# Input splits first, sums of squares last, at the start of a decoder-step kernel

## The reference

```
xn = rmsnorm(x, norm1_g)
z = einsum('btd,de->bte', xn, w_in)
rg_x, rg_y, q, k, v, g_lr, g_out, m_a, m_b = split(z)
```

## Time and profile before

| | |
|---|---|
| three runs, median | 1937.57 us |
| lowest and highest of them | 1936.34 and 1939.11 us |
| the profiled execution | 1936.35 us |
| its span in the profile | 1934.5 us |
| TensorE busy | 1901.1 us |
| VectorE, ScalarE, GpSimd busy | 925.8, 563.5, 41.7 us |

### The profile page before, as it was taken

The page is one execution under the profiler, slowest core; times in us unless marked ns, Lnnn a source line. Parts: engine busy times, 40 slices in busy tenths (PEclk is TensorE's granted clock), DMA queues, the critical chain, the costliest instruction groups (busy, mean ns, idle before and its releaser), DMA issues. The chain is left out here.

```text
span 1934.5 us, 28895 instructions
## 1 busy us (share of the span) xinstructions
PE 1901.1 (98%) x11890; PEld 1872.9 (97%) x11890; DVE 925.8 (48%) x1063; ACT 563.5 (29%) x627; POOL 41.7 (2%) x30
## 2 busy tenths in 40 slices
PE   7999999999999999999999999999999999999997
PEld 6999899999999999999999999999999999999997
DVE  5221277778854222332244455545453545454556
ACT  4010255665542111211132332222121212121215
POOL 2000000000000000000000000000000000000033
PEclk9999999999999999999999999999999999999998
DMA  5221123222211111311131111111111111111112
GB/s 195 88 91 44 44 68 135 99 81 97 93 66 43 44 54 43 132 44 43 50 136 44 56 45 46 53 45 44 45 44 46 53 45 44 44 44 55 44 52 88
DMA packets 48169, 127.13 MB, mean 66 GB/s; under 512 B 6952, under 2 KB 20008, under 8 KB 48080
## 3 DMA queue, kind: packets, MB, share of 16 engines
q1 hardware_dynamic: 27744, 88.39, 13.4%
q10 hardware_dynamic: 20352, 37.64, 5.5%
HBM read 108.14 MB, written 18.14 MB: 65 GB/s over the span
## 5 line engine op out<-in xcount | busy, mean ns | idle before, releaser
L414 PE MATMUL acc<-xn_hi,w_hi 128*128 128x346 f32 (+1 forms) x2520 | 551.6, 327 | 16.4 <-DVE xn_lo L1172 12.4
L414 PE MATMUL acc<-xn_lo,w_hi 128*128 128x346 f32 (+1 forms) x2520 | 540.2, 323 | 0.0
L414 PE MATMUL acc<-xn_hi,w_lo 128*128 128x346 f32 (+1 forms) x2520 | 538.9, 322 | 0.0
L414 PEld LDWEIGHTS acc<-xn_hi,w_hi 128*128 128x128 f32 x2520 | 425.8, 190 | 22.2 <-issue 13.3
L414 PEld LDWEIGHTS acc<-xn_lo,w_hi 128*128 128x128 f32 x2520 | 428.1, 189 | 0.0
L414 PEld LDWEIGHTS acc<-xn_hi,w_lo 128*128 128x128 f32 x2520 | 427.0, 189 | 0.0
L776 ACT ACTIVATE w_hi<-w_raw 128x1024 fp32r<-128x1024 f32 x147 | 154.3, 1050 | 468.5 <-PE acc L414 468.4
L1194 DVE TENSOR_TENSOR w_lo<-w_raw,w_hi 128x1024 fp32r<-128x1024 f32 x147 | 180.0, 1224 | 177.8 <-ACT w_hi L776 177.7
L1576 DVE TENSOR_TENSOR residual<-acc,residual 128x1032 f32<-128x1032 f32 x56 | 69.0, 1231 | 100.2 <-PE acc L414 100.2
L414 PE MATMUL acc<-act_hi,w_hi 128*128 128x344 f32 x504 | 108.2, 323 | 2.3 <-DVE residual L1576 2.3
L414 PE MATMUL acc<-act_hi,w_lo 128*128 128x344 f32 x504 | 107.6, 321 | 0.0
(11 more groups left out here) (218 smaller groups left out, 1990.6 us busy)
## 6 DMA issues: line engine op xcount, KB each, us to landing
w_raw<-in_w SPq DMA_DIRECT2D x153, 512.0 KB, 3.5
ha_scratch<-rg_gelu_ha ACTq DMA_DIRECT2D x8, 519.0 KB, 2.7
h<-ha_scratch ACTq DMA_DIRECT2D x8, 519.0 KB, 6.6
residual<-in_x ACTq DMA_DIRECT2D x8, 519.0 KB, 9.0
gla_qk_pair<-qk_scratch ACTq DMA_DIRECT2D x8, 512.0 KB, 4.5
smp_v_rows<-smp_v_scratch ACTq DMA_DIRECT2D x8, 512.0 KB, 5.7
out_gla_sample<-smp_state ACTq DMA_DIRECT2D x8, 512.0 KB, 3.2
smp_state<-in_gla_state ACTq DMA_DIRECT2D x7, 512.0 KB, 4.8
```

Of the source, the lines that this page charges most:

```text
L414: mm = nc.tensor.matmul(acc[g][:, n, 0:cw], w[s][:, t * P:(t + 1) * P], x[:, c0 + n * cw:c0 + (n + 1) * cw], start=a, stop=z)
```

## The change

Unit 0's transfer is cut in two, a head of two tiles (256 columns) with a semaphore of its own, and the rest, behind the parameters. Block 3 goes ahead of unit 1's weights. SyncE issues units 2 and 3 when units 0 and 1 are split, and only then the parameters and states. GpSimd's two splits are gone: ScalarE and VectorE split unit 1 behind block 2 and unit 2 in the middle of the squares. ScalarE does all eight high halves first, then squares into four buffers; VectorE does all eight low halves first, then the additions. After the fourth square ScalarE waits for unit 0, copies its 16 rows out of PSUM without the factor, which frees the bank, and splits unit 2's high half; VectorE multiplies the copy by the factor later, in place (`low_ready`). The sums over the partitions move back by one tile on TensorE. At the feed-forward's start, the residual's reload shares semaphores with the first load of the input.

The diff, without the declarations of semaphores:

```
@@ sync
-            sp.dma_start(raw[0], I["w"][0]).then_inc(w_loaded[0], 16)
+            sp.dma_start(raw[0][:, 0:HEAD], I["w"][0][:, 0:HEAD]).then_inc(head_loaded, 16)
             sp.dma_start(prm, I["params"]).then_inc(prm_loaded, 16)
+            sp.dma_start(raw[0][:, HEAD:], I["w"][0][:, HEAD:]).then_inc(w_loaded[0], 16)
             sp.dma_start(blk(X1, 1), I["x"][1]).then_inc(x_loaded[1], 16)
+            sp.dma_start(blk(X1, 3), I["x"][3]).then_inc(x_loaded[3], 16)
             sp.dma_start(raw[1], I["w"][1]).then_inc(w_loaded[1], 16)
-            for k in range(3, KB, 2):
+            for k in range(5, KB, 2):
                 sp.dma_start(blk(X1, k), I["x"][k]).then_inc(x_loaded[k], 16)
+            for s in range(2):
+                sp.wait_ge(w_split[s], 1)
+                sp.dma_start(raw[s], I["w"][2 + s]).then_inc(w_loaded[s], 16)
...
-            with sp.Fori(1, N_UNITS // 2) as i:
+            with sp.Fori(2, N_UNITS // 2) as i:
@@ gpsimd
-            split(0, 1)
-            split(1, 0)
@@ tensor
-                if k == 0:
+                if (g, k) == (0, 0):
+                    pe.wait_ge(head_split, 1)
+                elif (g, k) == (0, HEAD // P) or (g, k) == (1, 0):
                     pe.wait_ge(w_split[s], 1)
...
-                if (g, k) == (1, KB - 3):
+                if (g, k) == (1, KB - 2):
                     pe.wait_ge(sum1_done, KB)
                     norm_sum(xc, 0, sb6, sum1_mm)
                     norm_sum(xc, 1, sb7, sum1_mm)
-                if (g, k) == (1, KB - 2):
+                if (g, k) == (1, KB - 1):
                     pe.wait_ge(lnr1_done, 1)
                     norm_sum(xc, 2, sb6, sum1_mm)
...
-                pe.wait_ge(acc_free[0], 1)
+                pe.wait_ge(low_ready, 1)
                 zg_piece(0, NMETA, 0)
@@ scalar
-            act.wait_ge(w_loaded[0], 16)
-            nc.scalar.activation(whi[0], raw[0], ACT.Copy).then_inc(w_hi_done[0], 1)
+            act.wait_ge(head_loaded, 16)
+            nc.scalar.activation(whi[0][:, 0:HEAD], raw[0][:, 0:HEAD], ACT.Copy).then_inc(head_hi_done, 1)

             act.wait_ge(prm_loaded, 16)
             for k in range(KB):
                 act.wait_ge(x_loaded[k], 16)
                 nc.scalar.activation(blk(XH, k), blk(X1, k), ACT.Identity, scale=par("g1", k)).then_inc(xh1_done, 1)
-                if k >= 2:
-                    act.wait_ge(sum1_done, k - 1)
-                nc.scalar.activation((rt, it)[k % 2], blk(X1, k), ACT.Square).then_inc(sq1_done, 1)
+                if k == 0:
+                    act.wait_ge(w_loaded[0], 16)
+                    nc.scalar.activation(whi[0][:, HEAD:], raw[0][:, HEAD:], ACT.Copy).then_inc(w_hi_done[0], 1)
+                if k == 2:
+                    w_high(1)
+            for k in range(KB):
+                if k >= 4:
+                    act.wait_ge(sum1_done, k - 3)
+                nc.scalar.activation(sq1[k % 4], blk(X1, k), ACT.Square).then_inc(sq1_done, 1)
+                if k == 3:
+                    act.wait_ge(unit_done[0], 1)
+                    nc.scalar.activation(view3(glr[0:RANK]), acc[0][0:RANK, :, 0:NW], ACT.Copy).then_inc(acc_free[0], 1)
+                    w_high(2)
@@ vector
-            dve.wait_ge(w_hi_done[0], 1)
-            nc.vector.tensor_tensor(wlo[0], raw[0], whi[0].bitcast(F32), ALU.subtract).then_inc(w_split[0], 1)
+            dve.wait_ge(head_hi_done, 1)
+            nc.vector.tensor_tensor(wlo[0][:, 0:HEAD], raw[0][:, 0:HEAD], whi[0][:, 0:HEAD].bitcast(F32), ALU.subtract)\
+                .then_inc(head_split, 1)
...
             for k in range(KB):
                 dve.wait_ge(xh1_done, k + 1)
                 nc.vector.scalar_tensor_tensor(blk(XL, k), blk(X1, k), par("g1", k), blk(XH, k).bitcast(F32),
                                                ALU.mult, ALU.subtract).then_inc(xl1_done, 1)
+                if k == 0:
+                    dve.wait_ge(w_hi_done[0], 1)
+                    dve.wait_ge(head_split, 1)
+                    nc.vector.tensor_tensor(wlo[0][:, HEAD:], raw[0][:, HEAD:], whi[0][:, HEAD:].bitcast(F32), ALU.subtract)\
+                        .then_inc(w_split[0], 1)
+                if k == 2:
+                    w_low(1)
+            for k in range(KB):
                 dve.wait_ge(sq1_done, k + 1)
                 if k == 0:
-                    nc.vector.tensor_copy(xc, rt).then_inc(sum1_done, 1)
+                    nc.vector.tensor_copy(xc, sq1[0]).then_inc(sum1_done, 1)
                 else:
                     dve.wait_ge(sum1_done, k)
-                    nc.vector.tensor_tensor(xc, xc, (rt, it)[k % 2], ALU.add).then_inc(sum1_done, 1)
+                    nc.vector.tensor_tensor(xc, xc, sq1[k % 4], ALU.add).then_inc(sum1_done, 1)
+                if k == 3:
+                    w_low(2)
...
             dve.wait_ge(r1_done, 1)
-            evacuate(0, 0, 0, 0, glr[0:RANK, :], RANK)
+            dve.wait_ge(acc_free[0], 1)
+            nc.vector.tensor_tensor(glr[0:RANK, :], glr[0:RANK, :], rms[0:RANK, :], ALU.mult).then_inc(low_ready, 1)
```

More of the change, by code:

```diff
@@ L73 @@
 N_UNITS = U_FFN + UB + FB
+HEAD = 2 * P
 U_LAST = N_UNITS - GRP
@@ L200, in build @@
         sqsum = T[2]
+        sq1 = (rt, it, av, th)
         act_bytes = (2 * GRP * CB + 31) // 32 * 32
@@ L264, in build @@
         V3 = V.rearrange("p (k c) -> p k c", k=KB)
+        head_loaded, head_hi_done, head_split, low_ready = (
+            sem(n) for n in ("head_loaded", "head_hi_done", "head_split", "low_ready"))
         w_loaded, w_hi_done, w_split, unit_done = sems("w_loaded"), sems("w_hi_done"), sems("w_split"), sems("unit_done")
@@ L309, in build @@
         mgh_done, mgl_done = sem("mgh_done"), sem("mgl_done")
-        xr_loaded = sems("xr_loaded", KB)
         sq2_done, sum2_done, sum2_mm, lnr2_done, r2_done, xh2_done, xl2_done = (
@@ L774, in w_high @@
                 act.wait_ge(w_loaded[s], 16 * n + 16)
-                act.wait_ge(unit_done[s], n)
+                if u >= 2:
+                    act.wait_ge(unit_done[s], n)
                 nc.scalar.activation(whi[s], raw[s], ACT.Copy).then_inc(w_hi_done[s], 1)
@@ L1065, in _ @@
                     for m in range(KB):
-                        act.dma_start(blkl(X2, m), I["x"][m][:, late]).then_inc(xr_loaded[m], 16)
+                        act.dma_start(blkl(X2, m), I["x"][m][:, late]).then_inc(x_loaded[m], 16)
                 act.wait_ge(ma_done, KB if k == KB - 1 else k + 1)
@@ L1163, in plain, with w_low @@
                 dve.wait_ge(ones_done, 1)
-            dve.wait_ge(w_hi_done[0], 1)
-            nc.vector.tensor_tensor(wlo[0], raw[0], whi[0].bitcast(F32), ALU.subtract).then_inc(w_split[0], 1)
+            def w_low(u, per=0, i=0):
+                s, n = slot_of(u), nth(u, per, i)
+                dve.wait_ge(w_hi_done[s], n + 1)
+                nc.vector.tensor_tensor(wlo[s], raw[s], whi[s].bitcast(F32), ALU.subtract).then_inc(w_split[s], 1)
+            dve.wait_ge(head_hi_done, 1)
+            nc.vector.tensor_tensor(wlo[0][:, 0:HEAD], raw[0][:, 0:HEAD], whi[0][:, 0:HEAD].bitcast(F32), ALU.subtract)\
+                .then_inc(head_split, 1)
             dve.wait_ge(prm_loaded, 16)
@@ L1505, in _ @@
                 dve.wait_ge(unit_done[slot_of(U_OUT + k)], nth(U_OUT + k) + 1)
-                dve.wait_ge(xr_loaded[k], 16)
+                dve.wait_ge(x_loaded[k], 32)
                 nc.vector.tensor_tensor(view3(blkl(X2, k)), accl[g], view3(blkl(X2, k)), ALU.add).then_inc(acc_free[g], 1)
```

## The result

The median of 22 runs is **1940.72 us** (1939.38 to 1944.24) against 1936.33 us (1934.99 to 1939.39) for 22 runs of before. The ratio is 1.002, 95% interval [1.0014, 1.0026]: some 4 us slower. The interval lies clear of 1 and around the 0.2% at which the prediction drew the line between a change and none. The profiled execution took 1940.58 us, its span is 4.3 us longer than the one before.

A forecast was written before the change was run, and what follows sets the result against it. TensorE, busy for 98% of the span, was taken as the bound, so only its start before unit 2 and its clock count. Terms +1.1, +2.1 and +0.3 make +3.5 on 1936.35: 1939.9, stated as 1940.0 us, range 1936.5 to 1943.5.

The forecast's parts named there:

- The hole: Before the sums over partitions, TensorE stands still for 6.0 us, waiting for an 8.6 us chain from unit 0's end.
- The clock behind it: After the hole at the sums, TensorE runs at 1.2 GHz for a while, costing +2.1 us.
- the middle of two guesses, 1.3 and 3.0: Price of the low clock behind the hole: 1.3 lost at the first tile, about 3.0 at 227.57 to 234.39; +2.1 taken.
- The early clock: At the start, blocks 1 and 2 may run at 1.2 GHz behind a hole of some 2 us; +0.3 us taken.
- slack before 16.6: Half a microsecond to spare before unit 1's first tile at 16.6, deducted from the early tiles' 0 to 2.6 us.
- block 1 still lands near 9.4, perhaps later, as its queue is cut finer: At the start, input block 1 arrives about as before, leaving a hole of some 2 us behind the first tile.
- unit 0's gain: Unit 0 is complete at 31.4 in place of 34.13, 2.7 us earlier.
- rival 2: Slower: low clock at early tiles, unit 0 some 2 us later, and behind the hole, 3.0; 1942.6 us, chance 0.19.
- From unit 2 on the stream is solid, so a microsecond won or lost before it is one won or lost at the end: From unit 2 to the end, TensorE is busy throughout, so later waits are unchanged, cost 0.
- no change, on its slow side: Whole kernel: 1940.0 us, +2.4 us or 0.13% over the three-run median, within the 0.2% a measurement can tell.

The follow-up runs named there:

- e1: The changed kernel with the wait for unit 0, its copy and unit 2's split behind all eight squares (on VectorE, additions); 1936.58 us, ratio 0.9994 to before.
- e2: The changed kernel with 34 matmuls, their result overwritten, added on TensorE ahead of the wait for the sums; 1940.0 us, ratio 1.0016 to before.
- e3: The changed kernel with unit 0 loaded and split whole again, the rest as changed; 1942.9 us, ratio 1.0026 to before.
- e9: e4 with unit 1's weights ahead of block 3 again and 23 small warm-up matmuls ahead of the first tile; 1930.5 us, ratio 0.997 to before.
- e4: The changed kernel with the edits of e1 and e3 together; 1931.69 us, ratio 0.9975 to before.
- e5: e4 with 30 matmuls, their result overwritten, added in the sparse step in the middle; 1943.87 us, ratio 1.0034 to before.
- e8: e4 with unit 1's weights ahead of block 3 again, e5's added matmuls and 30 small ones ahead of the first tile; 1933.18 us, ratio 0.9978 to before.

## Why the prediction was right, and where it was not

**The hole, right.** From unit 0's end to the last addition's 33.42 to 41.90 = 8.48 us, forecast 8.6; hole 5.68, forecast 6.0; cause as said, shown by e1. Neither a wait on the low-rank rows nor one on late parameters took its place.

**The clock behind it, right.** Sums to unit 2 took 5.03 us where 2.8 was reckoned at full clock, so +2.2 for a forecast of +2.1; e2, with the clock up, puts it at 2.0. That the middle of two guesses, 1.3 and 3.0, came so close is luck in part; the mechanism is shown. The rule of the Trainium skill that was set beside this term ("TensorE: Matmul & The Clock Gate", Why this matters for your kernels), no idle gaps between bursts of matmuls, held here: 0.59 behind the hole, 1.00 in e2 without it.

**The early clock, wrong in size.** The forecast was +0.3, for tiles 2 and 3 that might run at 1.2 GHz but with slack before 16.6. They took 4.43 us, not 2.9, and started at 14.24. Unit 1's first tile came at 18.67 and not 16.6, so the term was **2.1 us** (e3 without the head: 16.54). The step that failed is "block 1 still lands near 9.4, perhaps later, as its queue is cut finer": it came at 11.58. Of the 2.1 us some 0.5 are this late start (14.24 + 2.9 is 17.1, not 16.6): the slack was used up. The other 1.5 are the clock at 1.2 GHz behind a hole of 2.98 us. With the 2.1 us unit 0's gain fell from 2.7 to 0.7 us (33.42 against 34.13). This is the first half of rival 2; its price for the second half, 3.0 behind the hole, was too high. Up to unit 2 the measured +5.3 lies nearer to rival 2's +6.2 than to the forecast's +3.5. (The prediction also calls the first tile's slow pace a slow clock. Its own row says 1.00 there; e9, where the tile runs at 0.72 us after 8 us of other matmuls, shows that the pace depends on what TensorE did before.)

**The middle, not foreseen.** "From unit 2 on the stream is solid, so a microsecond won or lost before it is one won or lost at the end" did not hold: a clock 0.05 higher between 215 and 245 gave 1.0 us back in the profiled execution. So the forecast of 1939.9 for that execution against its 1940.58 is partly luck: +1.8 at unit 2 (46.98 against 45.2), -1.0 in the middle. The forecast "no change, on its slow side" stands at its very edge, with an interval of 0.14 to 0.26%; its +0.13% was counted from the median of three runs, and against the 1936.33 of 22 runs the same 1940.0 is +0.19%.

## What to carry to other kernels

When work is regrouped on an in-order engine, look at which wait the last piece now stands behind: here half of the squares, ready to be made for 8 us, stood behind a wait for a unit that was not even due yet. Cut a transfer finer only if what is queued behind it has slack, and look at what a second queue gets meanwhile. Judge an edit of the start by the date of the event it should move (unit 2 here), not by the end time alone, which also carries the clock of a later stretch; but a lower clock that comes back in most executions, as in e3, is part of the edit's result until it is explained. Take a change apart when it loses: two of its parts cost 9 us, and without them the others were worth 4.6 over the kernel before.

## What was not expected of the hardware

- A sparse stretch of small matmuls near 225 us, with no standstill of TensorE longer than 1.9 us (before and e3), ran at a mean clock between 0.77 and 0.94 in the profiled executions of nearly equal kernels. The step took 13.9 us in e4 and 18.1 in e3, which is 4.2 of the 4.4 us between their rests (1891.5 and 1895.9). What decides it is open.
- Cutting one transfer of 512 KB in two made the next transfer of the queue reach its engine 2.1 us later (11.58 against 9.49 in e3), the bytes being the same; the blocks of the other queue landed 1.3 to 1.8 us sooner. Why the shares of the two queues shift is open.
- In e5's trace TensorE stood still behind two turns of a loop for 2.76 and 2.19 us with nothing to wait for, over 1100 us behind the added matmuls; e8, with more of them, stood 1.2 us at most. The Trainium skill says, in "Runtime: NRT & Kernel Launch" (Instruction fetch mechanics), that a taken branch to a target outside the two pages of instructions held forces a fetch. The trace agrees as far as one packet of the instruction queue falls into each of the two stalls; but e4 loads instructions at the first of these turns as well without such a stall, and no run here shows which engine's instructions a packet holds.
